# VectorE in place of GpSimd for the low halves of the weights in the SSD input projection

## The chip, the cores and the metric

The kernel runs on one core of one Trainium2 chip. The metric is the device time of one execution in microseconds, and lower is better. Five engines work side by side on a core, each through its own instruction queue: TensorE (PE, with its weight loads as PEld), VectorE (DVE), ScalarE (ACT), GpSimd (POOL) and SyncE (SP), which here issues DMAs. They order themselves only by semaphores.

## What is computed

Two transformer-like blocks run one after the other on 256 tokens of width 2048, in fp32. The change lies in the second block, in the mixer that the reference calls `_ssd_mixer`:

```
proj = h @ in_w
z, xBC, dt = jnp.split(proj, [SSD_D_INNER, SSD_D_INNER + SSD_CONV_DIM], axis=-1)
xBC = jax.nn.silu(_causal_depthwise_conv(xBC, conv_w, conv_b))
```

`xBC` has 6144 channels. The convolution runs over the tokens, with four taps per channel, each channel by itself: output token t is the weighted sum of the tokens t-3 to t, plus a bias. Silu follows. The other parts of the mixer (a scan over time, the product with silu of `z`, group norms and an output projection) need the finished `xBC`.

## The kernel before, in words

All weights come from HBM as fp32 tiles of 128 x 1024 (512 KB) in one stream, 258 bodies of four tiles. The table `STREAM` names the parts of the stream: the part `xbc` has 24 bodies, and `z` follows it. A tile lands in `raw[:, u, :]`, with u from 0 to 3 by its place in the body, and is split into two numbers of fewer bits: `w_hi` is a rounded copy, and `w_lo` is `raw - w_hi`. The activations `xt_hi` and `xt_lo` are split in the same way, and each product is done as three matmuls (high by high, low by high, high by low) in `three`.

So each tile goes through four queues, and `raw`, `w_hi` and `w_lo` have four places each, one for each u:

- SyncE (`weight`, L336 to L341) loads `raw` of place u once the low half of the tile that was there before is done (semaphore `lo_done`).
- ScalarE (`high`, L925 to L930) makes `w_hi`. It waits for the load, and for TensorE to have used the tile that was at this place one body earlier (`tile_used`). It raises `hi_done`.
- The low half is made by one of two functions of the same name `low`, that of GpSimd (L399 to L403) or that of VectorE (L1284 to L1288). It waits for `hi_done` and raises `lo_done`. In most parts of the stream this is VectorE's work. In `up0` and in `xbc` it is GpSimd's, through `lows` (L405 to L409).
- TensorE (`block_product`, L509 to L518) waits for `lo_done`, does the 24 matmuls of the tile and raises `tile_used`.

ScalarE and whichever engine makes the low half work one body ahead of TensorE: while TensorE works on body j, they make body j + 1.

In part `xbc` two tiles make one block b of 128 channels: 16 chunks of the model width are summed in PSUM bank b (`channel_blocks`, L520 to L525). A body has two blocks, b = 0 and b = 1. TensorE waits for `dve_free` before it starts a block, so that VectorE has read the block before last out of that bank. VectorE convolves each block (loop L1665 to L1674, `convolve` L1371 to L1379): one multiplication (L1373) and three multiply-and-add taps (L1377) into `cbuf[:, b, :]`, each waiting for the one before through the chain semaphore; then it raises `dve_free` and `conv_done`. ScalarE applies silu to it (`silu`, L1134 to L1138), which waits for `conv_done`.

The order of ScalarE in a body is written out by hand in L1140 to L1143: high 0, high 1, high 2, silu of block 0, high 3, silu of block 1. Two table loads stand in the same queue, one ahead of high 0 (recorded at L930), and one ahead of the silu of block 0 (recorded at L1137). Nothing in this queue is changed.

After the loop ScalarE raises `ssd_ready` (L1156), and only then GpSimd, VectorE and TensorE go on with the SSD scan. Before the loop VectorE works out `dt` (L1653 to L1663), some twenty small instructions one after another.

Part `rec`, early in the kernel, is one to compare with: there VectorE makes the low halves and does a convolution with four taps (L1400 to L1406), two low halves and then one block, while ScalarE makes high halves and nothing else.

Of the kernel before, what the change touches and what calls it, by code (L numbers as in the profile page):

```python
# [91 lines left out]
FIRST_BODY = {}  # L92
# [37 lines left out]
def build(nc, a, out):  # L130
    ctx = ExitStack()
    with ctx:
# [3 lines left out]
        def sb(name, shape, dt=F32, group=None):  # L136
            return (group or ctx).enter_context(nc.sbuf_tensor(name, shape, dt))
# [3 lines left out]
        def sem(name):  # L141
            if name not in names:
                names[name] = ctx.enter_context(nc.semaphore(name))
            return names[name]
# [106 lines left out]
        xbc = sb("xbc", [P, BC, S], F32, ssd)  # L251
# [108 lines left out]
        def _(pool):  # L360
# [38 lines left out]
            def low(body, u):  # L399

                pool.wait_ge(hi_done, 4 * body + u + 1)
                pool.tensor_tensor(w_lo[:, u, :], raw[:, u, :], w_hi[:, u, :].bitcast(F32), ALU.subtract)\  # L402
                    .then_inc(lo_done, 1)  # L403

            def lows(name):  # L405
                pool.wait_ge(lo_done, 4 * (FIRST_BODY[name] + 1))
                with pool.Fori(0, NB[name]) as j:
                    for u in range(4):
                        low(j + (FIRST_BODY[name] + 1), u)  # L409
# [37 lines left out]
            pool.wait_ge(sem("x3_done"), 1)  # L447
            pool.dma_start(w_dt[:, :, :], a["w_dt"]).then_inc(sem("w_dt_loaded"), 16)
            pool.dma_start(causal[:, :], a["causal"]).then_inc(sem("w_dt_loaded"), 16)
            lows("xbc")  # L450

            pool.wait_ge(sem("ssd_ready"), 1)
            with pool.Fori(0, SG) as g:
                pool.wait_ge(sem("xs_turned"), g + 1)
# [826 lines left out]
        def _(dve):  # L1281
            link = Chain(dve, dve_link)

            def low(body, u):  # L1284

                dve.wait_ge(hi_done, 4 * body + u + 1)
                dve.tensor_tensor(w_lo[:, u, :], raw[:, u, :], w_hi[:, u, :].bitcast(F32), ALU.subtract)\  # L1287
                    .then_inc(lo_done, 1)  # L1288
# [82 lines left out]
            def convolve(o, src, weight, centre):  # L1371

                link(dve.tensor_scalar(o, src, weight(centre), None, ALU.mult))  # L1373
                for t in range(4):
                    d = t - centre
                    if d < 0:
                        link(dve.scalar_tensor_tensor(o[:, -d:S], src[:, 0:S + d], weight(t), o[:, -d:S], ALU.mult, ALU.add))  # L1377
                    if d > 0:
                        link(dve.scalar_tensor_tensor(o[:, 0:S - d], src[:, d:S], weight(t), o[:, 0:S - d], ALU.mult, ALU.add))  # L1379
# [214 lines left out]
            for quarter in range(QUARTERS):  # L1594
                up, down = f"up{quarter}", f"down{quarter}"
                if quarter:
                    link(dve.memset(ada_acc[:, 1, :, :], 0.0))
                    with dve.Fori(0, 16) as j:
                        for u in range(4):
                            b = u // 2  # L1600
# [64 lines left out]
            with dve.Fori(0, NB["xbc"]) as j:  # L1665
                link.loop(j, 8)
                for b in range(2):
                    i = 2 * j + b
                    dve.wait_ge(tile_used, 4 * j + (4 * FIRST_BODY["xbc"] + 2 * b + 2))
                    dve.wait_ge(sem("conv_read"), i + 1)  # L1670
                    convolve(cbuf[:, b, :], PS[:, b, 0:S], lambda t: pc[:, ds(4 * i + (PC["a_conv_w"] + t), 1)], 3)
                    dve.sem_inc(dve_free, 1)  # L1672
                    dve.sem_inc(sem("conv_done"), 1)
# [56 lines left out]
            b = PC["ada_b"] + 84  # L1730
# [264 lines left out]
```

## Time and profile before

| what | value |
|---|---|
| median of 3 runs | 3893.26 us (3888.4 to 3894.15) |
| profiled execution: span, the only time the page gives of it | 3895.9 us |
| PE, PEld busy | 3431.8 us, 3096.4 us |
| DVE busy | 2303.0 us |
| ACT busy | 1692.7 us |
| POOL busy | 915.5 us |
| mean granted TensorE clock | 0.926 of full |
| DMA | 656.13 MB, mean 168 GB/s |

The profile is one execution. The share of busy time is a mean over stages with different limits, so the stage of the change is read by itself: part `xbc` runs from about 2380 to 2670 us of the span. Matmuls overlap in the pipeline: a matmul of 256 columns is listed with 0.28 us, while the next one starts 0.12 us later.

### The profile page before, as it was taken

To read this page: it belongs to the slowest core of one execution; us is meant where nothing else is said; L and a number is where in the kernel's file an instruction comes from. 1 tells how busy PE (TensorE), PEld (TensorE's weight loads), DVE (VectorE), ACT (ScalarE), POOL (GpSimd) and SP (SyncE) were. 2 spreads that over 40 slices of the span, in tenths; PEclk is the share of its full clock that TensorE was granted. 3 is DMA by queue.
4 is the path that set the end of the run, shared out by engine and by line. 5 is a ranking of instruction groups with operands and counts; after the bars stand their busy time and mean duration, and the time that the engine had idled before them with its cause. 6 is when DMAs were issued, how large, how long until landed. Compare 5 with 4: busy or idle time off the path is not lost.

```text
span 3895.9 us, 69368 instructions
## 1 busy us (share of the span) xinstructions
PE 3431.8 (88%) x23514; PEld 3096.4 (79%) x23514; DVE 2303.0 (59%) x3112; ACT 1692.7 (43%) x2243; POOL 915.5 (23%) x744
## 2 busy tenths in 40 slices
PE   7964899936999999999999997999998897998986
PEld 6953799925889888997799776998777686977975
DVE  4534549197678866896756664334555565444454
ACT  4434446512445543344434443665343344434443
POOL 1300008853123311431111113884111100000000
PEclk9967999956999999999999998999999898999998
DMA  6500444503866686667867772554443354554522
GB/s 199 166 22 32 162 163 156 174 14 97 265 205 209 194 264 213 215 214 236 265 205 250 244 252 72 184 181 154 144 142 121 126 193 141 178 173 146 182 98 87
DMA packets 181787, 656.13 MB, mean 168 GB/s; under 512 B 23040, under 2 KB 23184, under 8 KB 180576
## 3 DMA queue, kind: packets, MB, share of 16 engines
q1 hardware_dynamic: 149328, 545.82, 42.5%
q0 software_dynamic: 32400, 109.56, 9.3%
q8 instruction: 34, 0.56, 0.1%
q14 instruction: 25, 0.20, 0.0%
HBM read 653.18 MB, written 2.10 MB: 168 GB/s over the span
## 4 chain that ended last, share of the span: by engine, by line
PE 76%; DVE 9%; issue 7%; ACT 3%; POOL 3%; DVEq 1%; DMA 1%; ACTq 0%; POOLq 0%; SPq 0%; PEldq 0%
PE PS L505 12%; PE PS L506 12%; PE PS L507 12%; PE PS L557 9%; PE PS L561 9%; PE PS L559 9%; PE PS L540 2%; PE PS L542 2%; PE PS L541 2%; POOL w_lo L402 2%; POOL hot_gate_one L418 1%; PE PS L733 1%; PE PS L704 1%; PE PS L822 1%; PE PS L786 1%
## 5 line engine op out<-in xcount | busy, mean ns | idle before, releaser
L930 ACT ACTIVATE w_hi<-raw 128x1024 fp32r<-128x1024 f32 x1032 | 1093.2, 1060 | 1696.2 <-PE PS L507 944.9
L1287 DVE TENSOR_TENSOR w_lo<-raw,w_hi 128x1024 fp32r<-128x1024 f32 x872 | 1072.9, 1232 | 1006.7 <-ACT w_hi L930 1003.7
L505 PE MATMUL PS<-xt_hi,w_hi 128*128 128x256 f32 x4608 | 1327.5, 288 | 34.5 <-DVEq L1672 8.9
L506 PE MATMUL PS<-xt_lo,w_hi 128*128 128x256 f32 x4608 | 1313.2, 285 | 0.0
L507 PE MATMUL PS<-xt_hi,w_lo 128*128 128x256 f32 x4608 | 1312.3, 285 | 0.0
L505 PEld LDWEIGHTS PS<-xt_hi,w_hi 128*128 128x128 f32 x4608 | 893.8, 194 | 49.5 <-issue 36.1
L506 PEld LDWEIGHTS PS<-xt_lo,w_hi 128*128 128x128 f32 x4608 | 894.3, 194 | 0.0
L507 PEld LDWEIGHTS PS<-xt_hi,w_lo 128*128 128x128 f32 x4608 | 893.8, 194 | 0.0
L557 PE MATMUL PS<-w_hi,st_hi 128*128 128x512 f32 x1472 | 580.4, 394 | 40.5 <-DVE st_lo L1305 40.5
L559 PE MATMUL PS<-w_hi,st_lo 128*128 128x512 f32 x1472 | 578.9, 393 | 0.0
L561 PE MATMUL PS<-w_lo,st_hi 128*128 128x512 f32 x1472 | 578.1, 393 | 0.0
L402 POOL TENSOR_TENSOR w_lo<-raw,w_hi 128x1024 fp32r<-128x1024 f32 x160 | 402.1, 2535 | 241.7 <-ACT w_hi L930 241.7
L427 POOL DMA_DIRECT2D ada<-in_ada_w x336 | 181.7, 541 | 929.0 <-DVE ada_acc L1572 913.3
L557 PEld LDWEIGHTS PS<-w_hi,st_hi 128*128 128x128 f32 x1472 | 280.3, 190 | 100.5 <-issue 42.2
L561 PEld LDWEIGHTS PS<-w_lo,st_hi 128*128 128x128 f32 x1472 | 280.1, 190 | 59.3
L559 PEld LDWEIGHTS PS<-w_hi,st_lo 128*128 128x128 f32 x1472 | 280.4, 190 | 58.6
L1572 DVE SCALAR_TENSOR_TENSOR ada_acc<-ada,silu_c,ada_acc 128x512 f32<-128x512 f32 x336 | 250.2, 745 | 0.0
L418 POOL TENSOR_TENSOR hot_gate_one<-hot_one,slot_gate 128x512 bf16<-128x512 bf16 x64 | 120.7, 1887 | 165.6 <-DVE hot_one L1557 165.1
L540 PE MATMUL PS<-w_hi,xt_hi 128*128 128x512 f32 x352 | 139.4, 396 | 10.0 <-ACT v2n L1245 6.2
L541 PE MATMUL PS<-w_hi,xt_lo 128*128 128x512 f32 x352 | 138.6, 394 | 0.0
L542 PE MATMUL PS<-w_lo,xt_hi 128*128 128x512 f32 x352 | 138.6, 394 | 0.0
L494 POOL COPY q_st<-q2T 128x768 f32 x8 | 6.6, 828 | 538.9 <-PEq L870 499.1
(350 smaller groups left out, 3073.3 us busy)
## 6 DMA issues: line engine op xcount, KB each, us to landing
raw<-in_u_emb SPq DMA_DIRECT2D x256, 512.0 KB, 3.9
raw<-in_v_emb SPq DMA_DIRECT2D x256, 512.0 KB, 4.3
ada<-in_ada_w POOLq DMA_DIRECT2D x336, 256.0 KB, 3.7
raw<-in_xbc SPq DMA_DIRECT2D x96, 512.0 KB, 3.2
raw<-in_z SPq DMA_DIRECT2D x80, 512.0 KB, 3.2
raw<-in_q SPq DMA_DIRECT2D x64, 512.0 KB, 3.2
raw<-in_a_out SPq DMA_DIRECT2D x64, 512.0 KB, 4.2
raw<-in_k SPq DMA_DIRECT2D x48, 512.0 KB, 3.2
```

Source lines behind the costliest of these rows:

```text
L402: pool.tensor_tensor(w_lo[:, u, :], raw[:, u, :], w_hi[:, u, :].bitcast(F32), ALU.subtract)\
L505: pe.matmul(o, w_h, x_h, start=start, stop=False, skip_group_check=True)
L506: pe.matmul(o, w_h, x_l, start=False, stop=False, skip_group_check=True)
L507: return pe.matmul(o, w_l, x_h, start=False, stop=stop, skip_group_check=True)
L540: pe.matmul(o, xt_hi[:, k, t], w_hi[:, u, c:c + 512], start=k == 0, stop=False)
L541: pe.matmul(o, xt_lo[:, k, t], w_hi[:, u, c:c + 512], start=False, stop=False)
L557: pe.matmul(o, st_hi[:, s, t], w_hi[:, u, c], start=first and s == 0, stop=False, skip_group_check=True)
L559: pe.matmul(o, st_lo[:, s, t], w_hi[:, u, c], start=False, stop=False, skip_group_check=True)
L561: last = pe.matmul(o, st_hi[:, s, t], w_lo[:, u, c], start=False, stop=stop and s == 1, skip_group_check=True)
L930: act.activation(w_hi[:, u, :], raw[:, u, :], ACT.Copy).then_inc(hi_done, 1)
L1287: dve.tensor_tensor(w_lo[:, u, :], raw[:, u, :], w_hi[:, u, :].bitcast(F32), ALU.subtract)\
L1572: dve.scalar_tensor_tensor(acc[:, q, :], buffer[:, q, :], silu_c[:, ds(k, 1)], acc[:, q, :], ALU.mult, ALU.add).then_inc(sem("ada_used"), 1)
```

## The change

GpSimd no longer makes the low halves of part `xbc`. It goes from issuing the loads of `w_dt` and `causal` straight to its wait for `ssd_ready`. VectorE makes them, in the loop that convolves: in each body j, ahead of block b, the two low halves 2b and 2b + 1 of body j + 1. The taps, the queue of ScalarE, the matmuls and the loads are as they were.

```
@@ gpsimd, after the loads of w_dt and causal
-            lows("xbc")
-
             pool.wait_ge(sem("ssd_ready"), 1)
@@ vector, with dve.Fori(0, NB["xbc"]) as j:
                 link.loop(j, 8)
                 for b in range(2):
                     i = 2 * j + b
+                    for u in (2 * b, 2 * b + 1):
+                        low(j + (FIRST_BODY["xbc"] + 1), u)
                     dve.wait_ge(tile_used, 4 * j + (4 * FIRST_BODY["xbc"] + 2 * b + 2))
                     dve.wait_ge(sem("conv_read"), i + 1)
                     convolve(cbuf[:, b, :], PS[:, b, 0:S], lambda t: pc[:, ds(4 * i + (PC["a_conv_w"] + t), 1)], 3)
                     dve.sem_inc(dve_free, 1)
                     dve.sem_inc(sem("conv_done"), 1)
```

VectorE, the loop over the 24 bodies of `xbc`, from its head to the first tap of block 0, before (the rows marked ISA and REGISTER_ALU are register work and waits):

```order
L1665 UNCONDITIONAL_BRANCH
L1665 ISA
L1670 ISA
L1373 ISA
L1373 TENSOR_SCALAR cbuf<-PS,pc 128x256
L117 ISA
L1377 ISA
L1377 SCALAR_TENSOR_TENSOR cbuf<-PS,pc,cbuf 128x253
```

The same piece in the changed kernel, whose line numbers are lower by two:

```order
L1663 UNCONDITIONAL_BRANCH
L1663 ISA
L1285 TENSOR_TENSOR w_lo<-raw,w_hi 128x1024
L1284 REGISTER_ALU
L1285 TENSOR_TENSOR w_lo<-raw,w_hi 128x1024
L1669 ISA
L1670 ISA
L1371 ISA
L1371 TENSOR_SCALAR cbuf<-PS,pc 128x256
L117 ISA
L1375 ISA
L1375 SCALAR_TENSOR_TENSOR cbuf<-PS,pc,cbuf 128x253
```

Two operations of 128 x 1024 now stand ahead of the first tap.

VectorE, in the same loop, from the end of block 0 to the start of block 1, before:

```order
L1377 SCALAR_TENSOR_TENSOR cbuf<-PS,pc,cbuf 128x255
L117 REGISTER_ALU
L1669 REGISTER_ALU
L1670 REGISTER_ALU
L1373 ISA
L1373 TENSOR_SCALAR cbuf<-PS,pc 128x256
```

And in the changed kernel:

```order
L1375 SCALAR_TENSOR_TENSOR cbuf<-PS,pc,cbuf 128x255
L117 REGISTER_ALU
L1284 REGISTER_ALU
L1285 TENSOR_TENSOR w_lo<-raw,w_hi 128x1024
L1284 REGISTER_ALU
L1285 TENSOR_TENSOR w_lo<-raw,w_hi 128x1024
L1669 REGISTER_ALU
L1670 REGISTER_ALU
L1371 ISA
L1371 TENSOR_SCALAR cbuf<-PS,pc 128x256
```

Here low halves 2 and 3 stand between the last tap of block 0 and the first of block 1.

ScalarE, the whole body of its `xbc` loop in the changed kernel. But for the line numbers it is the body of before:

```order
L927 ISA
L928 ACT_TABLE_LOAD
L928 ACTIVATE w_hi<-raw 128x1024
L927 REGISTER_ALU
L928 ACTIVATE w_hi<-raw 128x1024
L927 REGISTER_ALU
L928 ACTIVATE w_hi<-raw 128x1024
L1134 ISA
L1135 ISA
L1135 ACT_TABLE_LOAD
L1135 ACTIVATE xbc<-cbuf,pc 128x256
L928 ACTIVATE w_hi<-raw 128x1024
```

High 3, the last row, stands behind the silu of block 0.

## Rows read from the trace of the kernel before

**Rows 1.** Page, section 1: busy time (share of the span) and instructions of each engine.

```profile
PE 3431.8 (88%) x23514; PEld 3096.4 (79%) x23514; DVE 2303.0 (59%) x3112; ACT 1692.7 (43%) x2243; POOL 915.5 (23%) x744
```

**Rows 2.** Busy time in one stretch inside `xbc`: engines, granted clock, DMA share, GB/s.

```profile
core 0: us, PE busy (x) PEld busy (x) DVE busy (x) ACT busy (x) POOL busy (x), PEclk, DMA share, GB/s
2410.00:2660.00 250.00, 250.00 (x2086) 250.00 (x2085) 83.62 (x174) 169.13 (x174) 206.02 (x87) 1.00 0.54 182
```

**Rows 3.** Groups of instructions in 2410 to 2660: busy, mean ns, idle before and releaser.

```profile
L402 POOL TENSOR_TENSOR w_lo<-raw,w_hi 128x1024 fp32r<-128x1024 f32 x87 | 206.8, 2409 | 44.0 <-ACT w_hi L930 44.0
L1377 DVE SCALAR_TENSOR_TENSOR cbuf<-PS,pc,cbuf 128x254 f32<-128x254 f32 x131 | 63.2, 482 | 19.0
```

**Rows 4.** Timeline of ACT at the loop's start: start us, us, what [idle before, releaser].

```profile
2399.91 1.28 ACT L1137 ACT_TABLE_LOAD   x1 [10.77 <-DVEq L1673]
2401.21 0.51 ACT L1137 ACTIVATE xbc<-cbuf,pc 128x256 f32 x1
2401.62 1.04 ACT L930 ACTIVATE w_hi<-raw 128x1024 fp32r<-128x1024 f32 x1
...
2413.31 0.51 ACT L1137 ACTIVATE xbc<-cbuf,pc 128x256 f32 x1
2413.88 1.06 ACT L930 ACTIVATE w_hi<-raw 128x1024 fp32r<-128x1024 f32 x1
2416.72 0.51 ACT L1137 ACTIVATE xbc<-cbuf,pc 128x256 f32 x1 [1.78 <-DVEq L1673]
2417.25 1.28 ACT L930 ACT_TABLE_LOAD   x1
2418.54 2.10 ACT L930 ACTIVATE w_hi<-raw 128x1024 fp32r<-128x1024 f32 x2
```

**Rows 5.** Timeline of DVE at the loop's start.

```profile
2397.18 0.48 DVE L1373 TENSOR_SCALAR cbuf<-PS,pc 128x256 f32<-128x256 f32 x1 [0.51 <-issue]
2397.84 0.48 DVE L1377 SCALAR_TENSOR_TENSOR cbuf<-PS,pc,cbuf 128x253 f32<-128x253 f32 x1 [0.17 <-DVE cbuf L1373]
2398.49 1.11 DVE L1377 SCALAR_TENSOR_TENSOR cbuf<-PS,pc,cbuf 128x254 f32<-128x254 f32 x2 [0.17 <-DVE cbuf L1377]
2400.15 0.48 DVE L1373 TENSOR_SCALAR cbuf<-PS,pc 128x256 f32<-128x256 f32 x1 [0.55 <-DVE cbuf L1377]
2400.78 1.73 DVE L1377 SCALAR_TENSOR_TENSOR cbuf<-PS,pc,cbuf 128x253 f32<-128x253 f32 x3
```

**Rows 6.** Timeline of DVE in part `rec`, low halves and taps on one engine.

```profile
170.84 1.22 DVE L1287 TENSOR_TENSOR w_lo<-raw,w_hi 128x1024 fp32r<-128x1024 f32 x1
171.98 0.48 DVE L1373 TENSOR_SCALAR convT<-PS,pc 128x256 f32 x1
...
173.95 0.48 DVE L1379 SCALAR_TENSOR_TENSOR convT<-PS,pc,convT 128x255 f32 x1 [0.15 <-DVE convT L1377]
174.59 0.35 DVE L1402 TENSOR_SCALAR convT<-convT,pc  x1 [0.15 <-DVE convT L1379]
175.17 1.23 DVE L1287 TENSOR_TENSOR w_lo<-raw,w_hi 128x1024 fp32r<-128x1024 f32 x1 [0.23 <-DVE convT L1402]
...
183.51 0.48 DVE L1373 TENSOR_SCALAR convT<-PS,pc 128x256 f32 x1
```

**Rows 7.** Timelines of ACT and DVE in part `a_out`, one high half and its low half.

```profile
3063.52 1.06 ACT L930 ACTIVATE w_hi<-raw 128x1024 fp32r<-128x1024 f32 x1 [1.66 <-PE PS L561]
...
3064.61 1.23 DVE L1287 TENSOR_TENSOR w_lo<-raw,w_hi 128x1024 fp32r<-128x1024 f32 x1 [1.49 <-ACT w_hi L930]
```

**Rows 8.** Timeline of DVE, then of PE, at the loop's two ends.

```profile
2668.10 1.74 DVE L1377 SCALAR_TENSOR_TENSOR cbuf<-PS,pc,cbuf 128x253 f32<-128x253 f32 x3
...
2399.79 0.58 PE L505 MATMUL PS<-xt_hi,w_hi 128*128 128x256 f32 x1 [8.87 <-DVEq L1672]
```

**Rows 9.** Page, section 6: DMA issues, KB each, median us from issue to landing.

```profile
raw<-in_xbc SPq DMA_DIRECT2D x96, 512.0 KB, 3.2
```

**Rows 10.** Busy time and granted clock in five stretches in and out of `xbc`.

```profile
100.00:105.00 5.00, 3.81 (x20) 3.81 (x21) 1.20 (x1) 2.13 (x2) 4.00 (x4) 0.66 0.54 195
2400.00:2405.00 5.00, 5.00 (x25) 5.00 (x26) 1.93 (x4) 4.44 (x5) 2.26 (x1) 0.51 0.00 0
2670.00:2675.00 5.00, 1.39 (x7) 1.39 (x8) 1.96 (x3) 1.73 (x7) 3.56 (x5) 0.61 0.60 202
2675.00:2680.00 5.00, 5.00 (x28) 4.16 (x27) 1.79 (x3) 2.40 (x4) 1.37 (x3) 0.71 0.53 158
3770.00:3775.00 5.00, 3.63 (x29) 3.31 (x28) 3.64 (x11) 4.10 (x7) 0.26 (x1) 1.00 0.00 0
```

**Rows 11.** Timeline of PE at about 100 us: the pause ahead of the low clock.

```profile
101.19 0.58 PE L505 MATMUL PS<-xt_hi,w_hi 128*128 128x256 f32 x1 [2.41 <-DVE w_lo L1287]
```

More of the change, by code:

```diff
@@ L449, in _ @@
             pool.dma_start(causal[:, :], a["causal"]).then_inc(sem("w_dt_loaded"), 16)
-            lows("xbc")
             pool.wait_ge(sem("ssd_ready"), 1)
@@ L1668, in _ @@
                     i = 2 * j + b
+                    for u in (2 * b, 2 * b + 1):
+                        low(j + (FIRST_BODY["xbc"] + 1), u)
                     dve.wait_ge(tile_used, 4 * j + (4 * FIRST_BODY["xbc"] + 2 * b + 2))
```

## The prediction

> **What bounds the kernel now.** The page comes first: TensorE is busy for 3431.8 of 3895.9 us, GpSimd for 915.5 [rows 1]. These are means over the whole kernel, so the second view is the busy time of one stretch inside part `xbc`. There TensorE is busy for all of 250.00 us at a clock of 1.00 and starts 2086 matmuls, one each 0.12 us [rows 2]. A tile has 24, so it takes 2.88 us, and a body of four tiles 11.5 us. Nothing else sets the pace there. GpSimd needs 2.41 us for a low half [rows 3], under the 2.88 us that TensorE gives it. A faster low half can therefore gain nothing in this part, and the question is only whether the new arrangement still delivers four tiles in each 11.5 us.
>
> The third view is the timeline, and it shows who waits for whom around the taps. Two things in it matter. The table load ahead of the silu of block 0 started at 2399.91, and what ended ScalarE's wait before it was VectorE's queue [rows 4]: the taps had ended at 2398.49 + 1.11 = 2399.60 [rows 5]. So the load is not done in advance; it stands behind the wait for the taps. And high 3 came behind that silu, at 2401.62 [rows 4]. Before the change this cost nothing, since the taps waited for TensorE alone.
>
> **The change, part by part.** Removed: 96 low halves of 2.41 us on GpSimd [rows 3]. They lie beside TensorE's work, so they are worth 0. GpSimd's next step waits for `ssd_ready`, which comes after the last silu in either kernel.
>
> Added: 96 low halves on VectorE, 1.23 us each and 1.14 us from the start of one to the start of what follows (171.98 - 170.84) [rows 6]. VectorE's own work in a body is 4 x 1.14 for the low halves, 2 x 2.42 for the taps (2397.18 to 2399.60 [rows 5]) and pauses of 0.23 and some 0.5 behind the taps [rows 5, 6]: 10.2 us. By itself that would fit into 11.5.
>
> What doesn't fit is the order. Low 3 waits for high 3; high 3 stands on ScalarE behind the silu of block 0; that silu waits for the taps of block 0; these now stand behind lows 0 and 1. Then the taps of block 1 stand behind low 3, their silu waits for them, and high 0 of the next body stands behind that silu. It is a ring through ScalarE and VectorE that nothing overlaps. One turn, from the start of high 0:
>
> - high 0, 1.06 [rows 4], and 0.03 to low 0 (3063.52 + 1.06 to 3064.61) [rows 7]: 1.09
> - lows 0 and 1, 2 x 1.14 [rows 6]: 2.28. High 1 ends at 2.1, just in time for low 1.
> - taps of block 0 [rows 5]: 2.42
> - to the table load, 2399.60 to 2399.91 [rows 4, 5]: 0.31
> - table load until silu, 2399.91 to 2401.21: 1.30
> - silu until high 3, 2401.21 to 2401.62: 0.41
> - high 3 and the hand-over: 1.09
> - low 3 until the first tap of block 1: 1.14
> - taps of block 1: 2.42, and 0.31 to its silu
> - silu until table load, 2416.72 to 2417.25: 0.53
> - table load until high 0 of the next body, 2417.25 to 2418.54 [rows 4]: 1.29
>
> The sum is 14.59 us, where TensorE needs 11.5. Low 2 follows the taps of block 0 within 0.23 us while ScalarE is still at its table load, so it is hidden; if that cover were gone it would cost 1.14. The loads: the place of a tile is free when its low half is done, its high half in the next body is over 9 us later at every place (low 2 ends at 7.3, high 2 of the next turn starts at 16.7), and a load takes 3.2 us [rows 9]. They stay hidden. TensorE starts a block 0.18 us after the taps that free its bank (2399.60 to 2399.79 [rows 5, 8]). It gets block 0 at 5.97 and block 1 at 12.64 of a turn, each 5.76 us of work, so it is idle for 3.1 us in a turn (0.9 ahead of block 1, 2.2 ahead of block 0) and never what ScalarE waits for.
>
> The start: the small instructions for `dt` hold VectorE until 2396.7 in either kernel. The first taps began at 2397.18 [rows 5]; now the first low half begins there. Highs 0 to 2 of that body are long done, so body 0 goes in at 1.09 of its turn, and the taps of its block 1 end at 2397.18 + 11.37 = 2408.55. With 23 more turns of 14.59 the last taps end at 2408.55 + 335.57 = 2744.1. Before they ended at 2668.10 + 1.74 = 2669.84 [rows 8]. What follows is unchanged and starts from these taps. The sum is **+74.3 us**.
>
> The bounds of the terms that the trace shows only nearby. The hand-over from a low half to taps is 1.14 in `rec`, with one wait ahead of the taps; here there are two, and behind other taps both took 0.55 from the end of the last instruction [rows 5], which would make 1.78. I take 1.14, as that row has the same pair of operations on the same engine. The other end adds 0.64 twice in a turn. Taps: 2.36 where VectorE had been ahead (2400.15 to 2402.51) [rows 5], 2.45 in `rec` (171.98 to 174.43) [rows 6]. From a silu: 0.41 to high 3, or 0.57 (2413.31 to 2413.88) [rows 4]. A turn lies between 14.35 (2.36 twice, and 0.41 in place of 0.53) and 16.09; in 24 turns that is 6 less and 36 more.
>
> The clock is the last term. After a pause of 2.41 us [rows 11] the granted clock was 0.66 over five us, and at 0.51 TensorE started only 25 matmuls in five us, 5 us for a tile in place of 2.88 [rows 10]: the lower level of 1.2 GHz. Elsewhere, at 3.63 us busy in 5, it stayed at 1.00 [rows 10]. Should the pause of 2 us in each turn bring the lower level for some 4 us, TensorE loses about 2 us in a turn, and it has 3 to spare. I take 0, and the granted clock of the stage may well be under 1. Behind the stage TensorE now waits some 12 us in place of 6, and restarts at a clock that was already 0.61 and 0.71 there [rows 10]: 0 to 2 us, taken as 0.
>
> A rule to weigh here concerns the table loads. The rows show 1.28 us for a load and silu 1.30 after its start, with nothing between [rows 4]. The Trainium skill, ScalarE: Activation LUTs, section "What ACT_TABLE_LOAD costs", counts a drain of about 1.38 us besides, 2.66 for each switch. If that drain were paid in this ring, a turn would be 2.8 longer. I go by the rows.
>
> The profiled span of 3895.9 is 2.6 above the median; the sum moves both alike: 3893.3 + 74 = **3967**.
>
> **The rivals.**
>
> *VectorE keeps up* (not slower). Part `rec` speaks for it: low halves and four taps and one more operation on the same engine, and its bodies still take 11.53 us (171.98 to 183.51) [rows 6]. VectorE's 10.2 us fit. Then only the two lows ahead of the first taps count, 2.3 us, and the time is 3896. It decides if the ring takes under 11.5 us. Against it: in `rec` ScalarE has no silu between its highs, and 3.1 us would have to leave the ring. 0.06.
>
> *The silu load runs ahead of the taps.* The other load does: it came 0.53 behind the start of silu 1 [rows 4]. Then the 1.30 falls out, a turn is 13.29, the last taps end at 2407.25 + 23 x 13.29 = 2712.9, and the time is 3893.3 + 43 = 3936. Against it: the load at 2399.91 waited although ScalarE had been idle for 10.77 us [rows 4]. 0.06.
>
> *Each load costs a pause besides*, longer than the rows show once ScalarE is pressed: 1.4 us more at two places in 24 turns, about 65 us: 4032. It is what the page named above would give. Against it: silu began 0.02 after the load. 0.04.
>
> *The clock stays at the lower level* through the stage: a tile takes 5 us [rows 10], a body 20, 8.5 over the present pace, 24 times: about 4100. Against it: TensorE without pause regained 1.00 within five us of the restart at 2399.79. 0.02.
>
> **How the numbers follow.** The forecast, the ring at 14.4 to 16.1 us, has 0.82, and its time is 3967. Its bounds are 3893 + 74 - 6 = 3961 and 3893 + 74 + 36 = 4003; the lowest run shown lies 5 under the median, which takes the lower end to 3956. That holds 0.82, so the range needs no other case. About 0.2% (8 us) is what a measurement can tell from no change. Slower: forecast and three rivals, 0.94. VectorE keeps up: 0.05 same, 0.01 faster.
>
> **What would show it.** In the changed profile: TensorE busy for about 80% of the stage, not all of it, and waiting for VectorE's queue (the raising of `dve_free`); the taps of block 0 follow each other at 14.6 us; VectorE waits for high 3 ahead of low 3, and ScalarE for VectorE ahead of both silus, with the table load behind the wait; the stage ends near 2744; GpSimd is busy for some 230 us less. The prediction is wrong if the taps come every 11.5 us, or if the table load stands ahead of the wait (13.3 us).

## The result: 1.6% slower, by the mechanism forecast and a little less of it

| | before | changed |
|---|---|---|
| median | 3893.7 us (3888.4 to 3895.26, 4 runs) | 3956.43 us (3948.16 to 3957.31, 4 runs) |
| span of the profiled execution | 3895.9 us | 3954.3 us |
| part `xbc`: first instruction of `dt` (L1655 before, L1653 after) to the clearing of `ada_acc_z` (L1691) | 293.6 us | 357.9 us |

The changed kernel takes 1.0155 times as long (95% interval 1.0141 to 1.017), some 60 us more, and 62.7 by the medians. Forecast were 74, from 63 to 110. So the direction and the order of size were right, and the time lay at the lower end of the range, by the ratio just below it.

The profile after, page, section 1 (to set beside [rows 1]):

```profile
PE 3441.0 (87%) x23514; PEld 3098.5 (78%) x23514; DVE 2408.2 (61%) x3208; ACT 1685.6 (43%) x2243; POOL 686.9 (17%) x648
```

GpSimd is busy for 229 us less and VectorE for 105 more: 96 low halves of 2.4 us went and 96 of 1.23 came. That would be 118 us more for VectorE; 6.2 are missing since some of its instructions became shorter (below), and most of the rest since busy time counts once what is listed with an overlap (a low half of 1.23 us has its follower begin 1.14 us after its start).

The changed kernel, busy time in three stretches inside `xbc`, to set beside [rows 2] (the columns are those of that group):

```profile
2410.00:2700.00 290.00, 247.34 (x1929) 240.41 (x1928) 169.82 (x240) 150.62 (x163) 0.00 (x0) 0.97 0.44 145
...
2425.00:2430.00 5.00, 5.00 (x34) 5.00 (x33) 3.06 (x5) 1.15 (x2) 0.00 (x0) 0.73 0.60 206
2430.00:2435.00 5.00, 5.00 (x44) 5.00 (x44) 2.30 (x3) 4.53 (x5) 0.00 (x0) 1.00 0.01 4
```

TensorE no longer fills the stage: 247 of 290 us, and VectorE with 170 doesn't either. No engine is at its limit. The first row counts 1929 matmuls in 290 us, 20.1 turns of 96, so 14.4 us a turn.

The waits in the same 290 us of the changed kernel (who waited for whom: us in total, times, longest):

```profile
DVE w_lo L1285 <- ACT w_hi L928: 95.4, 40, 3.2
ACT xbc L1135 <- DVEq L1673: 77.0, 20, 3.9
ACT L1135 <- DVEq L1673: 64.7, 21, 3.1
PEld PS L503 <- issue: 49.6, 35, 2.1
PE PS L503 <- DVEq L1672: 42.7, 35, 1.9
```

VectorE waits for ScalarE (highs 0 and 3, twice a turn), ScalarE for VectorE (the taps, twice a turn; the row without a tensor is the table load), and TensorE for VectorE's raising of `dve_free`. The ring can be followed through one turn. VectorE in the changed kernel, timeline:

```profile
2418.25 2.36 DVE L1285 TENSOR_TENSOR w_lo<-raw,w_hi 128x1024 fp32r<-128x1024 f32 x2 [3.23 <-ACT w_hi L928]
2420.53 0.47 DVE L1371 TENSOR_SCALAR cbuf<-PS,pc 128x256 f32<-128x256 f32 x1
2421.16 0.48 DVE L1375 SCALAR_TENSOR_TENSOR cbuf<-PS,pc,cbuf 128x253 f32<-128x253 f32 x1 [0.15 <-DVE cbuf L1371]
2421.78 1.11 DVE L1375 SCALAR_TENSOR_TENSOR cbuf<-PS,pc,cbuf 128x254 f32<-128x254 f32 x2 [0.15 <-DVE cbuf L1375]
2423.21 1.23 DVE L1285 TENSOR_TENSOR w_lo<-raw,w_hi 128x1024 fp32r<-128x1024 f32 x1 [0.31 <-DVE cbuf L1375]
2425.97 1.22 DVE L1285 TENSOR_TENSOR w_lo<-raw,w_hi 128x1024 fp32r<-128x1024 f32 x1 [1.54 <-ACT w_hi L928]
2427.11 0.48 DVE L1371 TENSOR_SCALAR cbuf<-PS,pc 128x256 f32<-128x256 f32 x1
2427.74 1.74 DVE L1375 SCALAR_TENSOR_TENSOR cbuf<-PS,pc,cbuf 128x253 f32<-128x253 f32 x3
2432.70 2.36 DVE L1285 TENSOR_TENSOR w_lo<-raw,w_hi 128x1024 fp32r<-128x1024 f32 x2 [3.23 <-ACT w_hi L928]
```

And ScalarE over the same turn:

```profile
2417.16 2.95 ACT L928 ACTIVATE w_hi<-raw 128x1024 fp32r<-128x1024 f32 x3
2423.19 1.28 ACT L1135 ACT_TABLE_LOAD   x1 [3.08 <-DVEq L1673]
2424.49 0.51 ACT L1135 ACTIVATE xbc<-cbuf,pc 128x256 f32 x1
2424.90 1.04 ACT L928 ACTIVATE w_hi<-raw 128x1024 fp32r<-128x1024 f32 x1
2429.79 0.51 ACT L1135 ACTIVATE xbc<-cbuf,pc 128x256 f32 x1 [3.85 <-DVEq L1673]
2430.32 1.28 ACT L928 ACT_TABLE_LOAD   x1
2431.61 2.95 ACT L928 ACTIVATE w_hi<-raw 128x1024 fp32r<-128x1024 f32 x3
```

A turn is 2431.61 - 2417.16 = 14.45 us. The hand-overs are those of the sum: high 0 starts at 2417.16, low 0 1.09 later, taps of block 0 2.28 behind it and done at 2422.89, table load at 2423.19 (0.30 later, behind the wait), silu 1.30 after its start, high 3 0.41 after that, low 3 at 2425.97 (1.07), taps of block 1 1.14 later, silu at 2429.79 (0.31 behind their end), table load 0.53 after it, high 0 1.29 after that.

### The profile page after: what moved, and what is told of

It reads as the page before. It is cut to its first block, busy times and chain, and to the rows that moved or that the text cites. A ratio compares the mean times of both kernels' runs of the same rounds, so it can differ in the third digit from the quotient of the medians.

```text
span 3954.3 us, 69319 instructions
## 1 busy us (share of the span) xinstructions
PE 3441.0 (87%) x23514; PEld 3098.5 (78%) x23514; DVE 2408.2 (61%) x3208; ACT 1685.6 (43%) x2243; POOL 686.9 (17%) x648
## 4 chain that ended last, share of the span: by engine, by line
PE 68%; issue 11%; DVE 11%; ACT 5%; POOL 3%; DVEq 1%; DMA 1%; ACTq 0%; POOLq 0%; SPq 0%; PEldq 0%
PE PS L503 10%; PE PS L504 9%; PE PS L505 9%; PE PS L555 9%; PE PS L559 9%; PE PS L557 9%; PE PS L538 2%; PE PS L540 2%; PE PS L539 2%; DVE cbuf L1375 2%; ACT w_hi L928 2%; POOL w_lo L402 2%; POOL hot_gate_one L418 1%; PE PS L731 1%; PE PS L702 1%
## 5 line engine op out<-in xcount | busy, mean ns | idle before, releaser
L1285 DVE TENSOR_TENSOR w_lo<-raw,w_hi 128x1024 fp32r<-128x1024 f32 x968 | 1189.7, 1232 | 1122.5 <-ACT w_hi L928 1112.1
L402 POOL TENSOR_TENSOR w_lo<-raw,w_hi 128x1024 fp32r<-128x1024 f32 x64 | 173.4, 2721 | 147.1 <-ACT w_hi L928 147.1
L702 PE MATMUL PS<-hot_gate_two,hot 128*128 128x64 bf16 x768 | 46.1, 240 | 97.0 <-DVE hid L1577 88.1
```

## The experiments

All medians are compared with runs of the kernel before on the same chip. "xbc" stands for the stretch of the table above, from `dt` to the clearing of `ada_acc_z`.

### Taps first on VectorE

```
                 for b in range(2):
                     i = 2 * j + b
-                    for u in (2 * b, 2 * b + 1):
-                        low(j + (FIRST_BODY["xbc"] + 1), u)
                     dve.wait_ge(tile_used, ...)
                     ...
                     dve.sem_inc(sem("conv_done"), 1)
+                    for u in (2 * b, 2 * b + 1):
+                        low(j + (FIRST_BODY["xbc"] + 1), u)
```

> The changed kernel with one swap on VectorE: in each half of a body the taps of block b come first, then low halves 2b and 2b + 1. All instructions are the same. Theory A (the ring through the queues of ScalarE and VectorE paces the stage, not the amount of work): now the taps of block 0 wait for low 3 of the body before and no longer for high 0, and low 3 no longer waits behind taps of block 0 that wait for high 0. The ring opens, VectorE's 10.2 us fit under TensorE's 11.5, and the taps of block 0 follow each other at 11.5 us. The start comes some 6 us sooner than in the kernel before, as the instructions for dt took 11.2 us in place of 17.4: 3886 to 3892 us. Rival B (VectorE now has too much to do in this stage, whatever the order): the same work on the same engine, so 14.5 us a body and about 3956 us.

Measured: 3886.71 us, 0.9986 of before (0.9977 to 0.9995). Busy time inside `xbc` of this kernel:

```profile
2410.00:2650.00 240.00, 240.00 (x2003) 240.00 (x2002) 179.29 (x250) 162.48 (x167) 0.00 (x0) 1.00 0.56 181
```

VectorE does the same instructions, more of them per microsecond than in the changed kernel (busy for 179 of 240 us, there for 170 of 290), and TensorE never waits in this stretch. The order was the cause, not the amount: rival B is out. The timeline of VectorE shows what it waits for now:

```profile
2546.97 0.48 DVE L1371 TENSOR_SCALAR cbuf<-PS,pc 128x256 f32<-128x256 f32 x1 [0.85 <-PE PS L505]
2547.59 1.74 DVE L1375 SCALAR_TENSOR_TENSOR cbuf<-PS,pc,cbuf 128x253 f32<-128x253 f32 x3
2549.66 2.36 DVE L1285 TENSOR_TENSOR w_lo<-raw,w_hi 128x1024 fp32r<-128x1024 f32 x2 [0.33 <-DVE cbuf L1375]
...
2558.48 0.48 DVE L1371 TENSOR_SCALAR cbuf<-PS,pc 128x256 f32<-128x256 f32 x1 [0.84 <-PE PS L505]
```

The taps of block 0 start when TensorE has finished the block, each 11.51 us, and the low halves follow without a wait for ScalarE, since their high halves were made meanwhile.

### High 3 ahead of the silu of block 0

```
                 for u in range(4):
                     high(j + FIRST_BODY["xbc"] + 1, u)
-                    if u >= 2:
-                        silu(u - 2)
+                for b in range(2):
+                    silu(b)
```

> The changed kernel with one swap on ScalarE: high 3 ahead of the silu of block 0. Theory A: low 3 follows low 2 at once. From the end of the taps of block 0 to the start of low 3 there were 3.08 us; now 0.31 and one low half of 1.14, so 1.45. The ring stays closed through silu 1 and high 0, and a turn is 14.46 - 1.63 = 12.83 us. 23 turns and a half: 38 us less than the changed kernel, 3918 us. Rival B (the amount of VectorE's work): unchanged, about 3956. Rival C (high 3 behind silu 0 is the whole cause): back to TensorE's 11.5 us a body, under 3893.

Measured: 3917.06 us, 1.0062 of before (1.0046 to 1.0077), 39 us less than the changed kernel. Timeline of VectorE:

```profile
2543.64 2.36 DVE L1285 TENSOR_TENSOR w_lo<-raw,w_hi 128x1024 fp32r<-128x1024 f32 x2 [3.23 <-ACT w_hi L928]
...
2556.47 2.36 DVE L1285 TENSOR_TENSOR w_lo<-raw,w_hi 128x1024 fp32r<-128x1024 f32 x2 [3.23 <-ACT w_hi L928]
```

A turn is 12.83 us, as worked out. The ring is shorter and still closed: the wait of 3.23 us ahead of low 0 is there, the one ahead of low 3 has gone. So theory A holds and rival C, which made high 3 the whole cause, does not.

### Both table loads out of the loop

```
             act.sem_inc(sem("conv_read"), 2)
+            act.activation(stat[0:SHEADS, 15:16], pc[0:SHEADS, PC["a_log"]:PC["a_log"] + 1], ACT.Silu)
             with act.Fori(0, NB["xbc"]) as j:
```

> The changed kernel with one tiny silu (64 x 1, its result unused) ahead of the loop on ScalarE: the loop is entered with the table set of silu, and both table loads leave the loop. Theory A: each was in the ring. From the taps of block 0 to low 3: 1.8 in place of 3.08 us; from the start of silu 1 to high 0: 0.41 in place of 1.82. A turn is 14.46 - 1.28 - 1.41 = 11.77 us, a little over TensorE's 11.5: about 3956 - 63 = 3893 us. Rival (table loads lie beside other work, ScalarE is busy only 184 of 365 us): 3956. If a load cost the engine a drain besides its 1.28 us, more would go than 2.7 us a turn, but TensorE's 11.5 is the floor; the trace would show it.

Measured: 3889.98 us, 0.999 of before (0.998 to 0.9999). Timeline of ScalarE in this kernel:

```profile
2546.87 2.01 ACT L928 ACTIVATE w_hi<-raw 128x1024 fp32r<-128x1024 f32 x2
2549.93 1.06 ACT L928 ACTIVATE w_hi<-raw 128x1024 fp32r<-128x1024 f32 x1 [1.06 <-PE PS L505]
2552.93 0.51 ACT L1136 ACTIVATE xbc<-cbuf,pc 128x256 f32 x1 [1.94 <-DVEq L1674]
2553.34 1.05 ACT L928 ACTIVATE w_hi<-raw 128x1024 fp32r<-128x1024 f32 x1
2558.24 0.51 ACT L1136 ACTIVATE xbc<-cbuf,pc 128x256 f32 x1 [3.85 <-DVEq L1674]
2558.66 2.01 ACT L928 ACTIVATE w_hi<-raw 128x1024 fp32r<-128x1024 f32 x2
```

High 0 comes at 2546.87 and 2558.66: a turn of 11.79 us, where 11.77 was expected. Two loads of 1.28 us and the 0.1 us of issue around them were worth 2.67 us a turn, though ScalarE was busy for only half of the stage. The `xbc` stretch is 297.6 us in place of 357.9, so they were worth 60.3 us in all (66.5 by the medians). The first full turn took 14.0 us: TensorE restarted after its pause of 4.3 us at a granted clock of 0.66, and ScalarE then waited for it three times in a row (1.8, 1.8 and 0.4 us). The ring is now just over TensorE's 11.5. The stretch is still 4.0 us longer than in the kernel before, while the median is 3.4 lower; the other stages make that difference, and it is not explained here.

### Taps first, and no table loads

The two edits above together.

> Taps first on VectorE and the tiny silu ahead of the loop together. Theory A: with the ring open TensorE paces the stage, so the 24 x 2 table loads that leave ScalarE's queue (62 us of its time) are worth nothing: the same as taps first alone, 3886.7 us within 0.2%. Rival: table loads cost time wherever they stand; then up to some tens of us less.

Measured: 3886.51 us, 0.9982 of before (0.9973 to 0.9991), against 3886.71 for taps first alone. The loads were worth some 60 us in the ring and are worth nothing beside TensorE. The `xbc` stretch is 289.2 us in both kernels.

### The kernel before, with GpSimd held until dt is done

This run tests the start of the stage, where the sum went wrong. It is made from the kernel before:

```
+            pool.wait_ge(sem("decay_done"), 1)
             lows("xbc")
```

> The kernel BEFORE with one wait: GpSimd starts the low halves of xbc only when VectorE has finished the instructions for dt. In the kernel before these took 17.4 us, beside three low halves of GpSimd; in the changed one 11.2 us, with GpSimd idle. Theory D (GpSimd's low halves hold up VectorE's instructions that read two operands from SBUF): dt takes 11.2 us, TensorE's pause at the start of xbc shrinks from 8.9 to some 3 us, and the time is 6 to 7 us less than before: 3887. Rival E (the 6 us come from something else than GpSimd, or the pause is bound by another wait): dt stays at 17.4 us or the time stays at 3893, or it is longer, since the low halves of the second body now start later.

Measured: 3888.42 us, 0.9988 of before (0.9979 to 0.9997). Here are VectorE's instructions for `dt` in the kernel before, beside three low halves of GpSimd (timeline of DVE):

```profile
2383.32 0.42 DVE L1363 TENSOR_TENSOR dtt<-dtt 64x256 f32<-64x256 f32 x1
2383.78 2.38 DVE L1364 TENSOR_SCALAR dtt<-dtt 64x256 f32<-64x256 f32 x1
2386.19 7.28 DVE L1366 SCALAR_TENSOR_TENSOR dtt<-dtt 64x256 f32<-64x256 f32 x7
```

And GpSimd in the same stretch of the kernel before:

```profile
2383.47 2.54 POOL L402 TENSOR_TENSOR w_lo<-raw,w_hi 128x1024 fp32r<-128x1024 f32 x1 [36.28 <-ACT w_hi L930]
2386.34 2.53 POOL L402 TENSOR_TENSOR w_lo<-raw,w_hi 128x1024 fp32r<-128x1024 f32 x1 [0.34 <-ACT w_hi L930]
2389.22 2.62 POOL L402 TENSOR_TENSOR w_lo<-raw,w_hi 128x1024 fp32r<-128x1024 f32 x1 [0.35 <-ACT w_hi L930]
```

Of the seven instructions that the third row of VectorE sums up, narrower windows of the same timeline show the two long ones:

```profile
2386.64 2.51 DVE L1366 SCALAR_TENSOR_TENSOR dtt<-dtt 64x256 f32<-64x256 f32 x1
2389.63 2.48 DVE L1366 SCALAR_TENSOR_TENSOR dtt<-dtt 64x256 f32<-64x256 f32 x1
```

VectorE in the kernel of this experiment:

```profile
2382.30 0.28 DVE L1365 TENSOR_SCALAR dtt<-dtt 64x256 f32<-64x256 f32 x1
2382.62 3.13 DVE L1367 SCALAR_TENSOR_TENSOR dtt<-dtt 64x256 f32<-64x256 f32 x7
```

One instruction took 2.38 us in place of 0.28 and ended 0.15 us after GpSimd's low half did. Seven others took 7.28 us in place of 3.13: two of them 2.51 and 2.48, ending 0.28 and 0.27 us after the second and the third low half, and the others 0.42, as here. So each low half held one instruction. The whole of `dt` is 10.9 us here and 17.1 in the kernel before (start of its first instruction to start of its last; the texts on record count to the end of the last, 0.3 us more). TensorE's pause at the start of `xbc` is 2.6 us in place of 8.9, and the stretch is 286.6 us in place of 293.6. The expectation was 3887; the median is 1.4 above it, and 5.0 under that of the kernel before.

### The changed kernel, with GpSimd busy beside dt

```
+            for u in range(3):
+                pool.wait_ge(hi_done, 4 * (FIRST_BODY["xbc"] + 1) + u + 1)
+                link(pool.tensor_tensor(xd[:, :, :].rearrange("p t n -> p (t n)"), X[:, 0, 0:1024], X[:, 1, 0:1024], ALU.subtract))
             pool.wait_ge(sem("ssd_ready"), 1)
```

> The changed kernel, in which GpSimd does three subtractions of 128 x 1024 again beside VectorE's instructions for dt, at the same moments as in the kernel before (each behind the high half of tiles 0 to 2), but of two unrelated tensors into scratch that nobody reads. Theory D (GpSimd's operations hold VectorE's up): dt takes 17.4 us again in place of 11.2, all behind it comes 6 us later, about 3963 us. Rival E (in the kernel before something else slowed dt): 11.2 us, 3956.

Measured: 3956.66 us, 1.0168 of before (1.0155 to 1.0182). The profile shows the mechanism as plainly as that of the run above. Timeline of GpSimd:

```profile
2373.36 2.53 POOL L452 TENSOR_TENSOR xd<-X 128x1024 f32<-128x1024 f32 x1 [36.28 <-ACT w_hi L931]
```

And of VectorE:

```profile
2373.65 2.38 DVE L1365 TENSOR_SCALAR dtt<-dtt 64x256 f32<-64x256 f32 x1
2376.06 7.29 DVE L1367 SCALAR_TENSOR_TENSOR dtt<-dtt 64x256 f32<-64x256 f32 x7
```

The instructions are as slow as in the kernel before, on tensors that have nothing to do with VectorE's. `dt` takes 17.1 us and the `xbc` stretch 364.35 us, 6.4 more than the changed kernel's 357.94. The expected total of 3963 did not come: the medians are equal (3956.66 and 3956.43), and the ratio is 1.0168 against 1.0155, with intervals that overlap. So the total doesn't show the 6 us. What precedes the stretch differed by more between the two profiled executions: `dt` begins at 2369.1 us here and at 2378.2 in the changed kernel. The stretch is the better witness.

### The same, with GpSimd only filling

The subtraction is replaced by `pool.memset` of the same scratch.

> As the run before, but GpSimd fills the scratch with a constant three times, so it reads nothing from SBUF. If it is GpSimd's reading that holds VectorE up: dt stays at 11.2 us and the time at 3956. If any operation of GpSimd does: dt is longer by about the time of the fills that it meets.

Measured: 3954.29 us, 1.0159 of before (1.0143 to 1.0174). `dt` takes 11.4 us, 0.5 more than with GpSimd idle. Timeline of VectorE:

```profile
2382.86 0.78 DVE L1365 TENSOR_SCALAR dtt<-dtt 64x256 f32<-64x256 f32 x1
2383.67 3.12 DVE L1367 SCALAR_TENSOR_TENSOR dtt<-dtt 64x256 f32<-64x256 f32 x7
```

And of GpSimd:

```profile
2382.54 0.95 POOL L452 MEMSET xd<- 128x1024 f32 x1 [36.18 <-ACT w_hi L931]
2385.81 0.95 POOL L452 MEMSET xd<- 128x1024 f32 x1 [2.31 <-ACT w_hi L931]
```

The tensor-scalar instruction was held (0.78 in place of 0.28 us) by a fill that reads nothing; the seven instructions with two operands from SBUF ran past the second fill untouched (3.12 us). So these are held by a GpSimd operation that reads, and the tensor-scalar form by one that reads and by one that only fills. The Trainium skill, SBUF — State Buffer, section "Who interferes with whom", states just this rule: VectorE shares a pair of ports with GpSimd, which an instruction takes for its whole length; VectorE needs it in a two-port mode, or for a second SBUF input, then only against a GpSimd operation that reads. These rows agree: the tensor-scalar instruction took 2.38 us beside a subtraction and 0.78 beside a fill in place of 0.28, and two-input instructions took 2.5 in place of 0.42 beside a subtraction and 0.42 beside a fill. That the tensor-scalar instruction ran in a two-port mode no row shows.

## Why the prediction was right and wrong

**What bounds the kernel** (TensorE in `xbc`, a faster low half gains nothing in the steady state): right. With the ring open the pace is 11.51 us, as before.

**The ring**: right in every link, and this is what decides. A turn was worked out as 14.59 us and measured 14.45. The taps took 2.36 and 2.37 us in place of 2.42 each, and the high half's hand-over 1.07 in place of 1.09; why the taps are shorter here is not shown. From the first low half to the last taps that is 3.1 us. The bounds were less good: of the unknown hand-overs the near value held each time (1.14 from a low half to taps, 0.41 from silu to high 3), and the upper end of 36 us was never near.

**The start: the step that failed.** The prediction said that the small instructions for `dt` hold VectorE until 2396.7 "in either kernel". They didn't. GpSimd's low halves had slowed them by 6.2 us, and the change takes GpSimd away from there. The first taps came 13.4 us after the start of `dt`, 6.8 earlier than the forecast had them. The other 0.6 of these 6.8 is a hand-over: the forecast put the first low half where the first taps had begun, 0.51 us behind the end of `dt`, and it began at that end. The row was in the trace of before: 2.38 us for a tensor-scalar operation of 64 x 256 on VectorE, where its neighbours of the same size took 0.42, with GpSimd's low half beside it. I counted GpSimd's removed work as worth 0 because its results were not waited for, and did not ask what its presence cost others. The two terms, 6.8 and 3.1, make up (but for rounding) the 10.0 us between the 74.3 forecast for the last taps and the 64.3 measured.

**Behind the stage**: taken as 0, and the SSD scan after it (L1691 to the copy of `ones_r`) took 335.9 us in place of 338.4. It took 337.8 to 338.6 us in five of the experiments and 335.7 and 336.0 in the other two. What decides between the two was not tried. It and some 3 us elsewhere make the 58.4 us between the spans out of 64.3.

**The clock**: taken as 0, right. After a pause of 1.86 us the granted clock fell in the turn shown (0.73 over five us above), as it did in four later turns; after most pauses of that length it stayed at 1.00, and what tells them apart is not shown. TensorE did not wait before the next block and 1.20 us before the one after it, in place of 0.57 and 1.87 in a turn at full clock. So it used up time that it had to spare, and the turn stayed 14.45 us.

**The table loads.** Load and silu are 1.30 us apart in the ring too. The further drain of about 1.38 us that the Trainium skill counts for each switch (ScalarE: Activation LUTs, section "What ACT_TABLE_LOAD costs") would have given a turn of 17.2, as an estimate, and taking both loads out would then have saved 5.4 us a turn. The trace disagrees: the turn was 14.45, and it saved 2.67.

**The rivals**: that VectorE keeps up was wrong for the order chosen, and right for the other order of the same instructions. (Its work in a body adds up to 10.1 us, not 10.2, of the terms given; nothing hangs on it.) That the silu load runs ahead of the taps was wrong: the load waited 3.08 us a turn behind `conv_done`. The two others did not occur.

A version that is a little under both kernels came out of it: taps first, 3886.71 us, 0.14% under before (interval 0.05% to 0.23%) and 1.8% under the changed kernel. Holding GpSimd back in the kernel before comes to about the same (3888.42 us).

## What to carry to other kernels

Adding up an engine's work tells whether it fits, not whether it arrives: when work is moved onto an engine that already trades results with another in a fixed order, write down the ring, link by link, with table loads and hand-overs, and compare one turn with the pace. If it is longer, look first for an order in which each engine does the work that is waited for before the work that only has to be ready later. And when work is taken off GpSimd, look for instructions of VectorE that are longer than their neighbours of the same size beside it.

## What the runs showed of the hardware

- A subtraction of 128 x 1024 on GpSimd held one VectorE instruction until it had ended: a tensor-scalar one (2.38 us in place of 0.28), and in two later cases one that reads SBUF twice (2.51 and 2.48 in place of 0.42). A fill of GpSimd held only the tensor-scalar one (0.78). Nothing in the kernel's semaphores shows this, and the profile lists it as busy time of VectorE.
- A table load stood behind the wait of the activation that it serves, in each of 24 turns, even with ScalarE idle for 3.08 us before it. It left the loop when an activation of the same set was placed ahead of the loop.
- TensorE at 14.45 us a turn, with pauses of up to 1.9 us, fell to the lower clock in five of 24 turns and lost nothing by it.
